# Layer two's softmax weights: transposed by VectorE and POOL's transfers in place of TensorE

## The chip, the cores and the metric

One NeuronCore of one Trainium2 chip runs the kernel. The metric is the device time of one execution in microseconds. Engines: TensorE (PE in the rows, its weight loads PEld), VectorE (DVE), ScalarE (ACT), GpSimd (POOL) and SyncE (SP), each with a queue that it runs in order; they wait for each other on semaphores. L12 is line 12 of the kernel before.

## What is computed

Two layers of a decoder over 256 positions, 2048 features and 16 heads of 128. Layer one has stick-breaking attention, layer two softmax attention against keys and values that are projected behind layer one. With 256 positions and blocks of 256 there is only a query's own block, so layer two's attention is plain causal softmax:

```python
def moba_layer(x, w_in, w_out, k, v, k_mean, pos):
    q, z = jnp.split(x @ w_in, 2, axis=-1)
    o = moba_attention(rope(split_heads(q), pos), k, v, k_mean)
    return (merge_heads(o) * jax.nn.silu(z)) @ w_out
...
        s_own = jnp.where(own_pos[None, :] <= t_idx[:, None], s_own, NEG_BIG)
...
        probs = jax.nn.softmax(scores, axis=-1).astype(v.dtype)
...
        x = layer_norm(DEEPNORM_ALPHA * x + y, ln_g[i], ln_b[i])
        x = x + (p[i] @ w_ple[i]) * jax.nn.sigmoid(x @ w_ple_gate[i])
```

Everything is float32 in and out.

## The kernel before

**Pieces.** All weights stream through the core as pieces of 256 rows by 512 columns (512 KB). SP loads a piece into one of 4 tiles of `raw`; ScalarE rounds it to `w_hi` (`split`, L481), VectorE subtracts to get `w_lo` (L752), both with 8 tiles; TensorE multiplies it in three passes, high by high, high by low, low by high, so twelve matmuls of 128x512 (L1191 to L1193). A chunk is eight pieces, one output of 512 columns, that is four heads; it goes to one half of `acc`, even and odd chunks in turn.

**Slots.** On ScalarE and VectorE `pieces` writes the program of a chunk as eight slots. Slot j first waits until TensorE has used piece j, then splits the piece eight further on; what else must be done at that time stands behind it (`after`) or ahead of it (`before`). SP's load into a tile of `raw` waits until VectorE's low half of the piece four earlier is done. TensorE's own steps stand behind the piece with the same number.

**Layer two's attention.** After the first K chunk come, for each group of four heads, a V chunk and the K chunk of the next group (`w_kv`); the last group's second chunk is the first eight pieces of the output projection (six of column block 0, then two of block 1; the remaining two of block 0 are pieces 12 and 13, of which piece 12 waits for the last group's gated rows). For a group, in order:
- V chunk, behind piece 2: TensorE turns the rotated keys (`k_turn_b`, waits `roped` and `gated`); ScalarE and VectorE copy them as high and low half (L525, L526, L1139).
- Behind pieces 4 and 5: `query_scores` for heads 0 and 1, then 2 and 3. The queries of tile 0 must have been copied to `qT` by POOL (L462).
- `row_max` (mask L790, maximum L1114), `softmax_exp` (L577), `divide` (L1123, L1127) on VectorE, ScalarE, VectorE, for two heads at a time (b = 0 and 1).
- K chunk, behind pieces 0 and 1: `probs_turn` transposes the probabilities with six 128x128 transposes for each b (L1400); ScalarE copies them out of PSUM (`probsT_copies`, L586, L587), VectorE makes the low half (`probs_lo`, L1149).
- Behind pieces 3 and 4: `weigh_values` for b = 0 and 1, three passes and a float32 matmul for the late keys (L1227, L1267).
- VectorE's slot 4: `gate_group` (L829), then, after ScalarE's `gated_hi` (L494), `gated_lo` (L767). Slot 5: `queries_hi_b` and `queries_lo_b` of the next group (L530, L1134).
- VectorE's slot 7: `k_end`, the rotation of the keys just projected, four products and two sums (L1050 to L1061).

**POOL's exchanges.** Elsewhere in the kernel (layer one's queries, keys and gates, layer two's queries, gates and normed rows) a transpose of a 128x1024 tile is made in two steps: VectorE transposes all its 32x32 squares (L773, L1067), and POOL moves the squares' blocks between groups of 32 partitions with 16 transfers (`exchange`, L431). At the end of layer two's attention POOL also starts the reload of the residual (`load_res(1, x2_spill)`, L401), after the last `q_lo`.

## Time and profile before

| | before |
|---|---|
| median of 3 executions | 1143.97 us (1143.33 to 1145.35) |
| the profiled execution, its own time | 1144.15 us |
| its span on the core | 1142.4 us |
| TensorE busy | 1137.7 us (100%) |
| VectorE busy | 746.5 us (65%) |
| ScalarE busy | 590.4 us (52%) |
| POOL busy | 232.7 us (20%) |
| TensorE's granted clock | 1.00 |

The time is that of the whole execution, the span that from the first to the last instruction. A share of busy time is an average over stages; matmuls overlap, so the start of one and of the next say more than its duration. A row of the timeline has the start in us from the span's start, the duration in us, engine, line, operation, what it writes and reads, and in brackets the idle time ahead of it with what ended it.

### The profile page before, as it was taken

The page shows a single profiled execution, that of the slowest core. Times are in us where ns is not written, and L with a number is a line of the kernel's source. Part 1 is how long each engine was busy: PE and PEld are TensorE (multiplying, and loading weights), DVE is VectorE, ACT ScalarE, POOL GpSimd, SP SyncE. Part 2 cuts the span into 40 slices and gives each one's busy share as a digit, 9 for nine tenths or more (in the row PEclk, how much of TensorE's full clock was granted, in tenths as well). Part 3 has the DMA queues.
Part 4 walks back from the last instruction along what each step waited for, and adds up shares of the span by engine and source line. Part 5 has one row for each costly group of instructions (what it writes and reads, how often), then busy time and mean ns, then how long its engine had stood idle before and what let it go on. Part 6 is the DMA issues. An engine that isn't in the chain of part 4 may idle for free.

```text
span 1142.4 us, 15523 instructions
## 1 busy us (share of the span) xinstructions
PE 1137.7 (100%) x5270; PEld 950.4 (83%) x5270; DVE 746.5 (65%) x795; ACT 590.4 (52%) x669; POOL 232.7 (20%) x475
## 2 busy tenths in 40 slices
PE   9999999999999999999999999999999999999998
PEld 8888888888888888888888888888888888888887
DVE  6665556556556566688798775457766667656873
ACT  6574556456546453455354555555454444434641
POOL 1402221330240300003537754320000010000000
PEclk9999999999999999999999999999999999999999
DMA  9776775675675686457787877764555575763671
GB/s 328 251 229 194 212 203 170 204 217 170 182 225 177 202 310 210 135 176 233 242 280 232 254 241 218 225 212 148 175 171 178 165 239 170 256 200 114 192 245 66
DMA packets 126587, 235.67 MB, mean 206 GB/s; under 512 B 13856, under 2 KB 16160, under 8 KB 126032
## 3 DMA queue, kind: packets, MB, share of 16 engines
q1 hardware_dynamic: 109888, 209.22, 58.5%
q0 software_dynamic: 16368, 25.37, 6.8%
q8 instruction: 24, 0.39, 0.1%
q10 hardware_dynamic: 288, 0.52, 0.1%
q14 instruction: 19, 0.16, 0.0%
HBM read 216.71 MB, written 4.19 MB: 193 GB/s over the span
## 4 chain that ended last, share of the span: by engine, by line
PE 100%; DVE 0%; POOL 0%; issue 0%; DVEq 0%; POOLq 0%
PE acc L1191 31%; PE acc L1193 31%; PE acc L1192 31%; PE aux L1227 2%; PE aux L1220 1%; PE aux L1253 1%; PE aux L1267 1%; PE aux L1284 0%; PE aux L1400 0%; PE aux L1193 0%; PE aux L1192 0%; PE aux L1191 0%; PE aux L1242 0%; PE aux L1389 0%; DVE stage L1038 0%; PE aux L1365 0%
## 5 line engine op out<-in xcount | busy, mean ns | idle before, releaser
L752 DVE TENSOR_TENSOR w_lo<-raw,w_hi 128x1024 fp32r<-128x1024 f32 x388 | 470.2, 1222 | 329.3 <-ACT w_hi L481 328.5
L481 ACT ACTIVATE w_hi<-raw 128x1024 fp32r<-128x1024 f32 x388 | 408.9, 1058 | 437.1 <-PE acc L1193 359.3
L1191 PE MATMUL acc<-w_hi,act 128*128 128x512 f32 x1548 | 607.7, 393 | 0.0
L1193 PE MATMUL acc<-w_hi,act 128*128 128x512 f32 x1548 | 603.1, 390 | 0.0
L1192 PE MATMUL acc<-w_lo,act 128*128 128x512 f32 x1548 | 602.5, 389 | 0.0
L1193 PEld LDWEIGHTS acc<-w_hi,act 128*128 128x128 f32 x1548 | 290.5, 188 | 61.6
L1191 PEld LDWEIGHTS acc<-w_hi,act 128*128 128x128 f32 x1548 | 290.8, 188 | 59.0 <-DVE act L767 0.3
L1192 PEld LDWEIGHTS acc<-w_lo,act 128*128 128x128 f32 x1548 | 290.8, 188 | 58.6
L431 POOL DMA_DIRECT2D heads<-big x192 | 93.8, 497 | 275.2 <-DVE big L773 232.1
L431 POOL DMA_DIRECT2D heads<-v_or_z x64 | 31.2, 497 | 52.0 <-DVE v_or_z L773 39.1
L431 POOL DMA_DIRECT2D stage<-v_or_z x48 | 23.6, 499 | 71.9 <-DVE v_or_z L990 44.5
L431 POOL DMA_DIRECT2D heads<-stage x64 | 31.4, 498 | 18.1 <-DVE stage L1079 16.5
L431 POOL DMA_DIRECT2D heads<-heads x64 | 32.1, 510 | 6.3 <-DVE heads L1067 6.1
L416 POOL TENSOR_TENSOR rstd<-var_eps,minus_half 128x2 f32<-128x2 f32 x3 | 2.2, 717 | 142.2 <-DVE var_eps L927 142.2
L494 ACT ACTIVATE act<-stage 128x1024 fp32r<-128x1024 f32 (+1 forms) x12 | 12.7, 1061 | 32.5 <-DVE stage L947 32.5
L462 POOL COPY heads<-big 128x512 f32 x4 | 2.5, 617 | 128.9 <-PE aux L1227 128.9
L577 ACT ACTIVATE heads<-aux,neg_max 128x128 f32<-128x128 f32 (+1 forms) x32 | 13.0, 420 | 23.7 <-DVE neg_max L1114 23.7
L767 DVE TENSOR_TENSOR act<-stage,act 128x1024 fp32r<-128x1024 f32 (+1 forms) x12 | 14.7, 1223 | 9.0 <-ACT act L494 9.0
L773 DVE STREAM_TRANSPOSE big<-acc 128x1024 f32<-128x1024 f32 x12 | 14.9, 1244 | 6.0 <-PE acc L1193 6.0
L947 DVE TENSOR_SCALAR stage<-aux,ln_col 128x256 f32<-128x256 f32 x32 | 15.2, 536 | 0.9 <-PE aux L1220 0.9
L494 ACT ACTIVATE act<-heads 128x1024 f32 (+1 forms) x8 | 8.5, 1062 | 11.7 <-DVE heads L829 11.7
L481 ACT ACT_TABLE_LOAD x9 | 11.5, 1283 | 4.8 <-DMA raw<-in_w_in_a 4.7
(158 smaller groups left out, 649.6 us busy)
## 6 DMA issues: line engine op xcount, KB each, us to landing
raw<-in_w_in_a SPq DMA_DIRECT2D x124, 512.0 KB, 3.9
raw<-in_w_ple_gate SPq DMA_DIRECT2D x64, 512.0 KB, 4.7
raw<-in_w_in_b SPq DMA_DIRECT2D x64, 512.0 KB, 4.7
raw<-in_w_kv SPq DMA_DIRECT2D x64, 512.0 KB, 3.7
raw<-in_w_out_a SPq DMA_DIRECT2D x32, 512.0 KB, 4.7
raw<-in_w_out_b SPq DMA_DIRECT2D x32, 512.0 KB, 4.8
heads<-big POOLq DMA_DIRECT2D x192, 32.0 KB, 3.3
heads<-in_ln_rows POOLq DMA_DIRECT2D x4, 1024.0 KB, 7.9
```

Source lines behind the costliest of these rows:

```text
L431: pool.dma_start(dst[g * SQUARE:(g + 1) * SQUARE, a * HT // NS:(a + 1) * HT // NS], src[a * SQUARE:(a + 1) * SQUARE, g * HT // NS:(g + 1) ...
L481: nc.scalar.activation(w_hi[:, r], raw[:, r % RAWS], ACT.Copy).then_inc(hi_ready, 1)
L494: nc.scalar.activation(quarter(dst[:, 0], c), src, ACT.Copy).then_inc(act_hi, 1)
L577: last = nc.scalar.activation(prob[:, b, h, lo:hi], aux_b[:, 2 * b + h, lo:hi], ACT.Exp, bias=neg_max[:, b, i:i + 1], accum_out=row_sum[:, ...
L752: nc.vector.tensor_tensor(w_lo[:, r], raw[:, r % RAWS], w_hi[:, r].bitcast(F32), ALU.subtract) \
L767: nc.vector.tensor_tensor(quarter(dst[:, 1], c), src, quarter(dst[:, 0], c).bitcast(F32), ALU.subtract).then_inc(act_ready, 1)
L773: nc.vector.transpose(turned_squares(dst), turned_rows(acc_of(parity))).then_inc(chunk_evac, 1)
L947: last = nc.vector.tensor_scalar(dst, part, g, b, ALU.mult, ALU.add)
L1191: nc.tensor.matmul(dst, hi, w_hi[:, r, i], start=begin, stop=False)
L1192: nc.tensor.matmul(dst, hi, w_lo[:, r, i], start=False, stop=False)
L1193: mm = nc.tensor.matmul(dst, lo, w_hi[:, r, i], start=False, stop=end)
L1227: mm = nc.tensor.matmul(dst, lhs(a), rhs(b), start=start and i == 0, stop=True, skip_group_check=True)
```

## The change

The six transposes for each b leave TensorE. VectorE transposes the divided probabilities as 32x32 squares into `probs_turned` (`turn_probs`, for b = 0 in slot 5, for b = 1 ahead of the split of slot 6), and POOL moves them with 16 transfers for each b into `probs_moved`, which lies where `prob` was; `probs_turned` lies over `kT` and half of `qT`. ScalarE rounds the early keys' weights for both b ahead of its split of the K chunk's slot 5 (`probs_hi`), VectorE subtracts there too (`probs_lo`). TensorE weighs for both b behind piece 6. Gate, high and low half, and the next group's queries, move to slot 7. The second two heads' `row_max` moves ahead of the split of slot 5. POOL copies the next group's queries to `qT` after both sets have landed, not after the scores.

```diff
--- before.py
+++ after.py
@@ -168,6 +168,9 @@
         qT = heads[:, HT:2 * HT].rearrange("p (h t) -> p h t", t=T)
         prob = heads[:, 2 * HT:2 * HT + 4 * SC].rearrange("p (b h c) -> p b h c", b=2, c=SC)
         gt = heads[:, 2 * HT + 4 * SC:].rearrange("p (h t) -> p h t", t=T)
+        PW = 2 * SC // (P // SQUARE)
+        probs_turned = [heads[:, b * 2 * SC:(b + 1) * 2 * SC] for b in range(2)]
+        probs_moved = [heads[:, 2 * HT + b * 2 * SC:2 * HT + (b + 1) * 2 * SC] for b in range(2)]
         gain = heads[:, 0:D]
         offset = heads[:, D:2 * D]
         NS = P // SQUARE
@@ -187,6 +190,16 @@
         def turned_squares(ap):
 
             return ap.rearrange("p (b h t c) -> p t h b c", b=NS, h=HG, t=TT)
+
+        probs_turned_x, probs_moved_x = ([squares(ap) for ap in aps] for aps in (probs_turned, probs_moved))
+
+        def probs_rows(b, lo, hi):
+
+            return prob[:, b, :, lo:hi].rearrange("p h (s a c) -> p h s a c", a=NS, c=SQUARE)
+
+        def early_keys(s, b):
+
+            return w1_parts[:, s, b].rearrange("p h (q a c) -> p (h q) a c", a=NS, c=SQUARE)
 
         vz_flat = v_or_z.rearrange("p t n -> p (t n)")
 
...
@@ -423,13 +437,13 @@
             pool.dma_start(cos_sin[:, :, :, :], rope).then_inc(tables_landed, 16)
             pool.dma_start(ln_col[:, :, :, :], ln_cols).then_inc(tables_landed, 16)
 
-            def exchange(turned, count, dst, src, moved):
+            def exchange(turned, count, dst, src, moved, width=HT // NS):
 
                 pool.wait_ge(turned, count)
                 for a in range(NS):
                     for g in range(NS):
-                        pool.dma_start(dst[g * SQUARE:(g + 1) * SQUARE, a * HT // NS:(a + 1) * HT // NS],
-                                       src[a * SQUARE:(a + 1) * SQUARE, g * HT // NS:(g + 1) * HT // NS]) \
+                        pool.dma_start(dst[g * SQUARE:(g + 1) * SQUARE, a * width:(a + 1) * width],
+                                       src[a * SQUARE:(a + 1) * SQUARE, g * width:(g + 1) * width]) \
                             .then_inc(moved, 16)
 
             for g in range(G):
@@ -457,13 +471,19 @@
                 pool.wait_ge(sz_ready, c + G)
                 exchange(chunk_evac, c + (C_Z + 1), gt_flat, vz_flat, z_moved)
             pool.wait_ge(qT_ready, 2 * G)
-            with pool.Fori(0, G) as g:
-                pool.wait_ge(scores_ready, g * 2 + 2 * G)
+            for g in range(G):
+                if g > 0:
+                    for b in range(2):
+                        exchange(p_turned, 2 * g - 1 + b, probs_moved[b], probs_turned[b], p_moved[b], PW)
+                    for b in range(2):
+                        pool.wait_ge(p_moved[b], g * MOVED)
                 nc.gpsimd.tensor_copy(qT[:, :, 0:P], quarter(q_all, g)[:, :, 0:P]).then_inc(q_group_ready, 1)
             pool.wait_ge(q_group_ready, G)
             pool.wait_ge(q_lo, 2 * G)
             pool.wait_ge(x2_spilled, 16 * G)
             load_res(1, x2_spill)
+            for b in range(2):
+                exchange(p_turned, 2 * G - 1 + b, probs_moved[b], probs_turned[b], p_moved[b], PW)
             pool.wait_ge(pv_done, 4 * G)
             load_p(1)
             pool.wait_ge(act_ready, S_OUT[1] + G)
@@ -579,12 +599,11 @@
                                                     accum_out=row_sum[:, b, i:i + 1])
                 last.then_inc(probs_raw, 1)
 
-            def probsT_copies(k, b):
-
-                act.wait_ge(probsT_psum, (k - G) * 2 + (b + 1))
-                s = scores_of(b)
-                nc.scalar.activation(prob[:, b, :, T:SC], s[:, :, T:SC], ACT.Copy).then_inc(w_ready, 1)
-                nc.scalar.activation(w1_parts[:, 0, b], s[:, :, 0:T], ACT.Copy).then_inc(weights_hi, 1)
+            def probs_hi(k, b):
+
+                act.wait_ge(p_moved[b], (k - G) * MOVED + MOVED)
+                nc.scalar.activation(early_keys(0, b), probs_moved_x[b][:, 0:4], ACT.Copy) \
+                    .then_inc(weights_hi, 1)
 
 
             for i, w_sem in enumerate((w_half_landed[0], w_landed[0])):
...
@@ -732,16 +751,19 @@
                 return {2: [lambda: k_copies_b(k)], 4: [lambda: softmax_exp(k, 0)],
                         5: [lambda: softmax_exp(k, 1)], 7: [lambda: values_hi_b(k, n + PC)]}
 
+            def before_k_b(k):
+                return {5: [lambda: probs_hi(k, 0), lambda: probs_hi(k, 1)]}
+
             def after_k_b(k):
-                return {0: [lambda: probsT_copies(k, 0)], 1: [lambda: probsT_copies(k, 1)],
-                        4: [lambda: gated_hi(k, k - G)]}
+                return {7: [lambda: gated_hi(k, k - G)]}
 
             with act.Fori(0, G - 1) as g:
                 n = g * (2 * PC) + (N_KV + PC)
                 pieces(n, N_KV, after_v_b(g + G, n))
-                pieces(n + PC, N_KV, after_k_b(g + G) | {5: [lambda: queries_hi_b(g + (G + 1))]})
+                pieces(n + PC, N_KV, {7: after_k_b(g + G)[7] + [lambda: queries_hi_b(g + (G + 1))]},
+                       before=before_k_b(g + G))
             pieces(N_OUT[1] - PC, N_KV, after_v_b(2 * G - 1, N_OUT[1] - PC))
-            out_ple_gate(1, after_k_b(2 * G - 1))
+            out_ple_gate(1, after_k_b(2 * G - 1), before_k_b(2 * G - 1))
 
 
         @block.vector
...
@@ -1129,6 +1152,14 @@
                         ALU.mult)
                 last.then_inc(probs_ready, 1)
 
+            def turn_probs(k, b):
+
+                dve.wait_ge(probs_ready, (k - G) * 2 + (b + 1))
+                nc.vector.transpose(probs_turned_x[b][:, 0:4].rearrange("p (h q) a c -> p h q a c", q=2),
+                                    probs_rows(b, 0, T))
+                nc.vector.transpose(probs_turned_x[b][:, 4:6], probs_rows(b, T, SC)[:, :, 0]) \
+                    .then_inc(p_turned, 1)
+
             def queries_lo_b(k):
                 dve.wait_ge(q_hi, k + 1)
                 nc.vector.tensor_tensor(q1_parts[:, 1], quarter(q_all, k - G)[:, :, P:T],
@@ -1146,29 +1177,33 @@
 
             def probs_lo(k, b):
                 dve.wait_ge(weights_hi, k * 2 + (b + 1))
-                nc.vector.tensor_tensor(w1_parts[:, 1, b], scores_of(b)[:, :, 0:T], w1_parts[:, 0, b].bitcast(F32),
-                                        ALU.subtract).then_inc(weights_lo, 1)
+                nc.vector.tensor_tensor(early_keys(1, b), probs_moved_x[b][:, 0:4],
+                                        early_keys(0, b).bitcast(F32), ALU.subtract).then_inc(weights_lo, 1)
 
             def after_v_b(k, n):
                 return {2: [lambda: keys_lo_b(k)],
-                        4: [lambda: row_max(k, 0)], 5: [lambda: row_max(k, 1), lambda: divide(k, 0)],
-                        6: [lambda: divide(k, 1)],
+                        4: [lambda: row_max(k, 0)], 5: [lambda: divide(k, 0), lambda: turn_probs(k, 0)],
                         7: [lambda: values_lo_b(k), lambda: evacuate_v(n, 1, v_or_z)]}
 
-            def after_k_b(k):
-                return {0: [lambda: probs_lo(k, 0)], 1: [lambda: probs_lo(k, 1)],
-                        4: [lambda: gate_group(k, k - G, quarter(sz_all, k - G)),
-                            lambda: gated_lo(k, k - G, (k - G) + S_OUT[1])]}
+            def before_v_b(k):
+                return {5: [lambda: row_max(k, 1)], 6: [lambda: divide(k, 1), lambda: turn_probs(k, 1)]}
+
+            def before_k_b(k):
+                return {5: [lambda: probs_lo(k, 0), lambda: probs_lo(k, 1)]}
+
+            def gate_b(k):
+                return [lambda: gate_group(k, k - G, quarter(sz_all, k - G)),
+                        lambda: gated_lo(k, k - G, (k - G) + S_OUT[1])]
 
             pieces(N_KV, N_KV, {5: [lambda: queries_lo_b(G)]} | k_end(N_KV, 0))
             with dve.Fori(0, G - 1) as g:
                 n = g * (2 * PC) + (N_KV + PC)
-                pieces(n, N_KV, after_v_b(g + G, n))
-                pieces(n + PC, N_KV, after_k_b(g + G) | {5: [lambda: queries_lo_b(g + (G + 1))]}
-                       | k_end(n + PC, g + 1))
+                pieces(n, N_KV, after_v_b(g + G, n), before=before_v_b(g + G))
+                pieces(n + PC, N_KV, {7: gate_b(g + G) + k_end(n + PC, g + 1)[PC - 1]
+                                      + [lambda: queries_lo_b(g + (G + 1))]}, before=before_k_b(g + G))
             n = N_OUT[1] - PC
-            pieces(n, N_KV, after_v_b(2 * G - 1, n))
-            out_ple_gate(1, after_k_b(2 * G - 1))
+            pieces(n, N_KV, after_v_b(2 * G - 1, n), before=before_v_b(2 * G - 1))
+            out_ple_gate(1, {7: gate_b(2 * G - 1)}, before_k_b(2 * G - 1))
 
 
         @block.tensor
...
@@ -1392,14 +1427,18 @@
                                       lambda i, h=h: k1_parts[:, i, h], False)
                 mm.then_inc(scores_ready, 1)
 
-            def probs_turn(k, b):
-
-                pe.wait_ge(probs_ready, (k - G) * 2 + (b + 1))
+            def weigh_values_b(k, b, v_chunk):
+
+                pe.wait_ge(weights_lo, k * 2 + (b + 1))
+                pe.wait_ge(v_lo, k + 1)
+                pe.wait_ge(chunk_evac, v_chunk + 1)
                 for i in range(2):
-                    for s in range(3):
-                        mm = nc.tensor.transpose(aux_b[:, 2 * b + i, s * P:(s + 1) * P],
-                                                 prob[:, b, i, s * P:(s + 1) * P], ident[:, :])
-                mm.then_inc(probsT_psum, 1)
+                    head = slice((2 * b + i) * P, (2 * b + i + 1) * P)
+                    o = aux_b[:, 2 * b, i * T:(i + 1) * T]
+                    three_passes(o, lambda part: v1_parts[:, part, head], lambda part: w1_parts[:, part, b, i], i == 0)
+                    mm = nc.tensor.matmul(o[:, P:T], v_or_z[:, 1, head], probs_moved_x[b][:, 4 + i], start=False,
+                                          stop=True, skip_group_check=True)
+                mm.then_inc(pv_done, 1)
 
             chunk(N_Q, N_Q, act1, 0, C_Q, quarters=S_X2, after={2: [last_x2_turn]})
             with pe.Fori(1, 2 * G) as c:
@@ -1410,9 +1449,7 @@
                         5: [lambda: query_scores(k, 1)]}
 
             def after_k_b(k, v_chunk):
-                return {0: [lambda: probs_turn(k, 0)], 1: [lambda: probs_turn(k, 1)],
-                        3: [lambda: weigh_values(k, 0, v_chunk, v1_parts, v_or_z, w1_parts)],
-                        4: [lambda: weigh_values(k, 1, v_chunk, v1_parts, v_or_z, w1_parts)]}
+                return {6: [lambda: weigh_values_b(k, 0, v_chunk), lambda: weigh_values_b(k, 1, v_chunk)]}
 
             chunk(N_KV, N_KV, act0, 0, C_KV, quarters=S_KV)
             pe.wait_ge(sz_ready, 2 * G)
```

Left out: the semaphores (`p_moved` and `p_turned` come, `probsT_psum` goes), the argument by which `out_ple_gate` takes `before_out`, and `weigh_values` of layer one, whose body stays.

The instructions of VectorE at the end of a K chunk, before. L752 is a split, L829 the gate, L767 the low half of the gated rows, L1050 to L1061 the rotation:

```order
L829 TENSOR_TENSOR heads<-aux,big 128x1024
L767 ISA [waits act_operand_hi]
L767 TENSOR_TENSOR act<-heads,act 128x1024
...
L752 TENSOR_TENSOR w_lo<-raw,w_hi 128x1024 [waits act_hi_ready]
L1050 TENSOR_TENSOR heads<-acc,cos_sin 128x8x64 [waits pe_piece_used]
L1051 TENSOR_TENSOR heads<-acc,cos_sin 128x8x64
L1052 TENSOR_TENSOR heads<-acc,cos_sin 128x8x64
L1053 TENSOR_TENSOR heads<-acc,cos_sin 128x8x64
L1058 ISA [waits dve_rope_mul]
L1059 TENSOR_TENSOR heads<-heads 128x8x64 [waits dve_chunk_evac]
L1061 TENSOR_TENSOR heads<-heads 128x8x64
```

And of the change, where L774 is the split, L851 the gate, L789 the low half, and from L1073 the rotation:

```order
L774 TENSOR_TENSOR w_lo<-raw,w_hi 128x1024 [waits act_hi_ready]
L851 ISA [waits pe_pv_done,act_sz_ready]
L851 TENSOR_TENSOR heads<-aux,big 128x1024
L788 REGISTER_ALU
L789 ISA [waits act_operand_hi]
L789 TENSOR_TENSOR act<-heads,act 128x1024
L1073 TENSOR_TENSOR heads<-acc,cos_sin 128x8x64 [waits pe_piece_used]
L1074 TENSOR_TENSOR heads<-acc,cos_sin 128x8x64
L1075 TENSOR_TENSOR heads<-acc,cos_sin 128x8x64
L1076 TENSOR_TENSOR heads<-acc,cos_sin 128x8x64
L1080 REGISTER_ALU
L1081 ISA [waits dve_rope_mul]
```

The gate and its low half, with the wait for ScalarE's high half (`act_operand_hi`) between them, stood behind the split of slot 4; now they stand behind that of slot 7, ahead of the rotation; the low half of the next group's queries (L1134, now L1165) follows behind the rotation.

POOL from the gates' exchanges on, before (the copy stands in a loop over the four groups):

```order
L431 DMA heads<-v_or_z 32x256 x64
L460 UNCONDITIONAL_BRANCH
L460 ISA
L462 ISA
L462 COPY heads<-big 128x4x128
L460 REGISTER_ALU
L460 COMPARE_AND_BRANCH
L401 DMA big<-x_spill 128x2x512 x4
L406 DMA stage<-in_pt 128x2x256
```

And of the change, its last two groups:

```order
L480 COPY heads<-big 128x4x128
L445 DMA heads<-heads 32x192 x32
L480 COPY heads<-big 128x4x128
L415 DMA big<-x_spill 128x2x512 x4
L445 DMA heads<-heads 32x192 x32
```

Two sets of 16 transfers now lie behind each copy (the first three pairs stand above these rows in the same way), and the reload of the residual (`big<-x_spill`) lies between the last copy and the last two sets.

TensorE in the K chunk, behind the last matmul of piece 6, in the change (the transposes behind pieces 0 and 1 and the weighing behind 3 and 4 are gone):

```order
L1228 MATMUL acc<-w_hi,act 128x512
L1432 ISA
L1434 REGISTER_ALU [waits dve_v_lo,dve_weights_lo]
L1262 MATMUL aux<-act,v_parts 128x256 [waits dve_chunk_evac]
L1262 MATMUL aux<-act,v_parts 128x256 x2
L1439 MATMUL aux<-heads,v_or_z 128x128
L1262 MATMUL aux<-act,v_parts 128x256 x3
L1439 MATMUL aux<-heads,v_or_z 128x128
L1432 REGISTER_ALU
L1262 MATMUL aux<-act,v_parts 128x256 [waits dve_chunk_evac,dve_v_lo,dve_weights_lo]
L1262 MATMUL aux<-act,v_parts 128x256 x2
L1439 MATMUL aux<-heads,v_or_z 128x128
```

Each of the two steps waits for the low half of its own two heads (`dve_weights_lo`); the second follows the first with no piece between.

## Rows read from the trace of the kernel before

**Rows 1.** The page, chain that ended last, by engine.
```profile
PE 100%; DVE 0%; POOL 0%; issue 0%; DVEq 0%; POOLq 0%
```

**Rows 2.** Windows, first group: us, engines' busy us (instructions), PEclk, DMA share, GB/s.
```profile
769.30:819.90 50.60, 50.60 (x254) 42.72 (x253) 34.79 (x42) 26.12 (x42) 0.61 (x1) 1.00 0.51 161
```

**Rows 3.** Timeline of PE: start us, us, engine, line, operation, tiles, shapes, count.
```profile
777.32 1.04 PE L1220 MATMUL aux<-ident,heads 128*128 128x128 f32 x8
...
793.97 0.39 PE L1193 MATMUL acc<-w_hi,act 128*128 128x512 f32 x1
...
796.69 0.39 PE L1193 MATMUL acc<-w_hi,act 128*128 128x512 f32 x1
...
796.92 0.82 PE L1400 MATMUL aux<-ident,heads 128*128 128x128 f32 x6
...
800.10 0.39 PE L1193 MATMUL acc<-w_hi,act 128*128 128x512 f32 x1
...
806.22 0.39 PE L1193 MATMUL acc<-w_hi,act 128*128 128x512 f32 x1
...
806.45 0.52 PE L1227 MATMUL aux<-act,v_parts 128*128 128x256 f32 x3
...
807.53 0.48 PE L1191 MATMUL acc<-w_hi,act 128*128 128x512 f32 x1
...
810.15 0.39 PE L1193 MATMUL acc<-w_hi,act 128*128 128x512 f32 x1
...
819.53 0.39 PE L1193 MATMUL acc<-w_hi,act 128*128 128x512 f32 x1
```

**Rows 4.** Timeline of DVE, then line L1067: duration ns min/median/max.
```profile
791.74 0.69 DVE L790 TENSOR_TENSOR aux<-aux,future 128x512 f32<-128x512 f32 x1
...
793.40 0.17 DVE L1123 RECIPROCAL row_sum<-row_sum 128x4 f32<-128x4 f32 x1
...
793.60 1.03 DVE L1127 TENSOR_TENSOR heads<-heads,row_sum 128x256 f32<-128x256 f32 x2
...
812.87 1.22 DVE L829 TENSOR_TENSOR heads<-aux,big 128x1024 f32<-128x1024 f32 x1
...
815.46 1.23 DVE L767 TENSOR_TENSOR act<-heads,act 128x1024 f32 x1 [1.37 <-ACT act L494]
...
821.11 1.23 DVE L752 TENSOR_TENSOR w_lo<-raw,w_hi 128x1024 fp32r<-128x1024 f32 x1 [1.49 <-ACT w_hi L481]
...
822.25 0.68 DVE L1050 TENSOR_TENSOR heads<-acc,cos_sin 128x512 f32<-128x512 f32 x1
...
825.37 0.68 DVE L1061 TENSOR_TENSOR heads<-heads 128x512 f32<-128x512 f32 x1
...
919.59 1.23 DVE L752 TENSOR_TENSOR w_lo<-raw,w_hi 128x1024 fp32r<-128x1024 f32 x1
...
L1067 DVE STREAM_TRANSPOSE heads<-heads x4: 1245/1245/1247, 601.5 to 666.7; 128x1024 f32<-128x1024 f32 x4
```

**Rows 5.** Timeline of POOL, then DMA issues: KB each, median us to landing.
```profile
689.12 7.81 POOL L431 DMA_DIRECT2D heads<-v_or_z  x16 [12.84 <-issue]
...
789.07 0.61 POOL L462 COPY heads<-big 128x512 f32 x1 [28.97 <-PE aux L1227]
...
920.22 2.88 POOL L401 DMA_DIRECT2D big<-x_spill  x4 [29.33 <-DVE q_parts L1134]
...
raw<-in_w_out_b SPq DMA_DIRECT2D x32, 512.0 KB, 4.8
...
heads<-heads POOLq DMA_DIRECT2D x64, 32.0 KB, 3.6
```

**Rows 6.** Timeline of ACT, then line L510: duration ns min/median/max.
```profile
700.42 1.28 ACT L560 ACT_TABLE_LOAD   x1 [0.73 <-DMA heads<-v_or_z]
...
930.72 1.06 ACT L481 ACTIVATE w_hi<-raw 128x1024 fp32r<-128x1024 f32 x1 [3.00 <-DMA raw<-in_w_out_b]
...
L510 ACT ACTIVATE big<-heads x4: 613/632/633, 66.0 to 348.3; 128x512 f32<-128x512 f32 x4
```

22 lines of the change are left out of this document (12 added, 10 removed).

## Prediction

> **What bounds the kernel now.** I read the chain of waits first: every part of it that counts is TensorE [rows 1]. Then the windows, one for each group of four heads in layer two: 50.60 us long, TensorE busy for all of it, at a granted clock of 1.00 [rows 2]. So whatever leaves TensorE's queue there shortens the run, and whatever makes TensorE wait there lengthens it, and nothing else counts. All other numbers come from the timelines of one group, from 769.3 to 819.9 us; a span of 50.60 us repeats it.
>
> In TensorE's timeline [rows 3] a piece of twelve matmuls takes 2.72 us (793.97 to 796.69). I call the V chunk's pieces V0 to V7 and the K chunk's K0 to K7; 793.97 is the last matmul of V7, 819.53 that of K7.
>
> **What leaves TensorE.** A piece with six transposes behind it takes 3.41 us (796.69 to 800.10), so six cost 0.69. The six behind K1 cost about the same. Eight such steps: 8 x 0.68 = 5.4 us saved, all on the path. The weighing stays, four steps of it less: a step costs 810.15 - 806.22 - 2.72 = 1.21 us, of which its own matmuls are 807.53 - 806.45 = 1.08; the other 0.13 is the passage back to wide matmuls, which two steps in a row pay once: 4 x 0.13 = 0.5 us saved. ScalarE and VectorE also lose or swap copies of equal size (two of 128x256 go, two of 128x512 move); that lies beside TensorE's work and is priced at nothing.
>
> **What is added beside it.** In each group VectorE gets two times a transpose of 128x512 and one of 128x256. The nearest row is 1.245 us for 128x1024 [rows 4]; by elements, with 0.18 us fixed, that is 0.71 and 0.45, about 1.04 us one after the other. VectorE has over 15 us idle in each window [rows 2], so only its place in the chain of the softmax matters. POOL gets 32 issues a group.
>
> **First wait: the weights must be back before the weighing.** I follow the chain in the first group's times.
> 1. The scores of the second two heads are there when POOL's copy wakes, 789.07 [rows 5]. VectorE now masks them and takes their maximum at once: 793.40 - 791.74 = 1.66 us [rows 4], so 790.7. Then the split of slot 5 (1.14, 821.11 to 822.25), the division of the first two heads (0.20 + 1.03) and the two transposes (1.04): 794.1.
> 2. POOL needs 16 issues for each set. One set took 7.81 us of issues [rows 5], two 15.65. It wakes some 0.5 us after a transpose has ended; so the last issue ends at about 810.4. The second two heads are transposed by 796.5, long before POOL can take them.
> 3. From the end of the last issue (689.12 + 7.81 = 696.93) to the reader's start at 700.42 [rows 5, 6] 3.5 us passed. The 3.6 us median from issue to landing [rows 5] gives 3.2. Where traffic is low it may be half of that. I take 3.0 (range 1.7 to 3.5): ScalarE starts at 813.4.
> 4. ScalarE rounds 128x512 in 0.63 [rows 6], VectorE subtracts in about 0.7, with some 0.1 us of signals twice: 815.0.
> TensorE wants the second step at 793.97 + 7 x 2.72 + 0.23 + 1.08 = 814.3. The first step is ready in time, as its set lands 8 us earlier. So TensorE stands still for 0.6 us in each group, 4 x 0.6 = 2.4 us in all; between 0 (1.7 us in point 3) and 1.2 each (3.5 us), so 0 to 4.8.
> The wait in front of slot 5 holds up ScalarE's splits behind it, three of them by up to 3 us, and VectorE's with them; these feed pieces eight later, 21.8 us, and reach nobody.
> A sentence apart: the Trainium skill, DMA: Bandwidth & Descriptors, section on the anatomy of a SWDGE transfer, fits 2.0 us plus bytes over 436 GB/s, which for 24 KB is 2.1 us; the trace has 3.6 for transfers of 32 KB, and the measurement decides. By the page's figure the first wait would vanish and the estimate would be 2.4 us lower.
>
> **Second wait: the gate is now in front of the rotation.** Call U the end of K7 (819.53 + 0.39 = 819.92). Before, VectorE split at 821.11, rotated the keys from 822.25 and was done at 825.37 + 0.68 = 826.05, so U + 6.1 [rows 4]. TensorE turns these keys behind V2, at 777.32 + 50.60 = 827.92, U + 8.0 [rows 3]. The margin was 1.9 us. The weighing behind K6 pushes gate and low half out of slot 4 into slot 7, ahead of the rotation. From the gate's start to that of the low half 2.59 us pass, in which VectorE waits for ScalarE's high half, then 1.14 for the low half itself [rows 4]: 3.7 us. The keys are rotated at U + 9.9. TensorE waits 1.9 us, and its weight load can't run ahead any more, 0.2: 2.1 us. It happens behind the K chunks of the first three groups (the very first K chunk has no gate ahead, and behind the fourth group nothing is rotated): 3 x 2.1 = 6.3 us lost. Bounds: 5.6 (no restart cost) and 6.9. Late next are the low halves of the turned keys, wanted behind V4; by the same addition they are ready at U + 15.1 where TensorE comes at U + 16.7: no further wait.
>
> **Third: what POOL has moved.** The 2 MB of the residual (four issues at 920.22 [rows 5], U - 0.9 of the third group) wait for the last low half of the queries, which now comes behind the rotation, U + 10.6. They now meet the weights for slots 4 and 5 of the last V chunk. Before, they delayed ScalarE by 3.00 us at 930.72 [rows 6], where the softmax was not yet running. Now the same squeeze lies on it. The raw tile for slot 4 is freed by the low half of slot 0, U + 11.6. At the usual 4.8 us from issue to landing [rows 5] it is there at U + 16.4, with a third more at U + 18; ScalarE wants it at U + 17.1. Before, the tile read at 930.72 had been freed at 919.59 + 1.23 = 920.82 [rows 4], 9.9 us earlier; at that rate it is U + 21.5. I take the nearer end, since this tile has no other queued in front of it: the last group's exponentials, set and weighing come 1.0 us later (0 to 4.4). POOL's copy of the queries now stands behind both sets (about 814), but its readers come behind V4 at about U + 16.7, over 20 us later.
>
> **The sum:** - 5.4 - 0.5 + 2.4 + 6.3 + 1.0 = + 3.8 us. The profiled execution took 1144.15 us around a span of 1142.4; the median is 1143.97, 0.2 below, and I put the sum on the median: **1147.8 us**. By the bounds alone, from - 5.9 + 5.6 = - 0.3 to - 5.9 + 4.8 + 6.9 + 4.4 = + 10.2.
>
> **Rivals.**
> - *The sets land quickly.* With 1.7 us from the last issue to the reader, the first wait is gone: 1147.8 - 2.4 = 1145.4. For it: a transfer is a quarter smaller than those of the rows. Against it: the weight stream runs at the same time, as it did at 700.42. The second wait is untouched.
> - *The last group is squeezed harder.* If the residual's 2 MB take the larger share and the raw tile of slot 4 lands 4.4 us late, as the 9.9 us in front of 930.72 make thinkable, the third term is 4.4 and not 1.0: 1147.8 + 3.4 = 1151.2.
> - *Faster: the rotation keeps its old place in time.* The mechanism of the second wait would have to fail: it decides at whether the rotated keys are signalled by U + 8.0. If VectorE could do gate and low half under waits that it has anyway, the sum is 3.8 - 6.3 = - 2.5, so 1141.5; with quick landings as well 1139.1. For it: VectorE is idle for a third of the window. Against it: in slot 7 there is no idle time ahead of the rotation, which followed the split directly (821.11, 822.25), and its engine runs in order.
> - *It doesn't give back the transposes.* If TensorE hides part of them in its pipeline, 5.4 shrinks; but the pieces' ends are 3.41 apart and not 2.72, so I give this next to nothing.
>
> **How the numbers follow.** My forecast 0.50, quick landings 0.20, harder squeeze 0.15, faster 0.12, the last 0.03. A measurement of this kernel can tell about 0.2% from no change, 2.3 us. Slower are the forecast, the squeeze and the last (0.50 + 0.15 + 0.03), less 0.03 for a forecast whose terms all fall low: 0.65. Within: quick landings (+ 1.4) and these 0.03, 0.23. Faster: 0.12. The range reaches from 1142.8, which leaves out most of the faster case, to 1151.4, which takes in the squeeze, and leaves out about 2 in 10.
>
> **What would show it.** TensorE idle, in the profile after, in front of the turning of the keys, about 2 us, three times, put down to VectorE's rotation; TensorE idle in front of the second weighing step of each group, 0.6 us, put down to VectorE's subtraction and behind that to POOL's transfers; windows of the middle groups 50.60 - 1.5 + 2.1 + 0.6 = 51.8 us long; the clock still 1.00. Window lengths of about 49.1 us would prove me wrong: then no wait was there. No idle time at the keys but a longer one at the weighing would mean that the sets, not the gate, are the price.

## The result, and the profile after

The changed kernel took **1153.69 us** (median of 6 runs, 1152.56 to 1155.86), the kernel before 1144.21 beside it: ratio 1.0085, 95% interval 1.0075 to 1.0095. It is 9.5 us slower. Forecast were + 3.8 us, with a range to 1151.4: the direction was right, the size wrong.

The page, where [rows 1] had TensorE for the whole chain:

```profile
span 1152.0 us, 15541 instructions
...
PE 1135.7 (99%) x5222; PEld 947.6 (82%) x5222; DVE 754.0 (65%) x811; ACT 588.4 (51%) x661; POOL 295.2 (26%) x603
...
PE 91%; POOL 3%; DVE 2%; DMA 2%; issue 1%; ACT 1%; DVEq 0%; ACTq 0%; POOLq 0%
```

The rest of the chain is now POOL's issues, VectorE and transfers. The windows, bounded where TensorE's steps stand (columns as in [rows 2]):

```profile
819.10:870.30 51.20, 49.37 (x242) 41.44 (x241) 36.73 (x46) 25.74 (x41) 16.23 (x33) 1.00 0.55 178
870.30:923.30 53.00, 49.59 (x242) 41.47 (x241) 36.73 (x46) 25.72 (x41) 16.23 (x33) 1.00 0.54 173
923.30:980.00 56.70, 50.42 (x235) 42.20 (x234) 36.71 (x46) 24.05 (x39) 19.27 (x37) 0.94 0.62 203
```

TensorE now has idle time in each: 1.8, 3.4 and 6.3 us. In the last the clock is 0.94. The waits of TensorE (us in total, times, longest) name two places:

```profile
PE aux L1262 <- DVE act L1180: 6.1, 2, 4.5
PE aux L1255 <- DVE heads L1084: 5.4, 3, 1.8
```

L1255 turns the keys, L1084 is the rotation's last sum; L1262 weighs, L1180 is the low half of the weights. TensorE's timeline at these places:

```profile
814.53 0.60 PE L1262 MATMUL aux<-act,v_parts 128*128 128x256 f32 x3
...
815.11 0.60 PE L1262 MATMUL aux<-act,v_parts 128*128 128x256 f32 x3
...
815.69 0.48 PE L1226 MATMUL acc<-w_hi,act 128*128 128x512 f32 x1
...
826.46 0.39 PE L1228 MATMUL acc<-w_hi,act 128*128 128x512 f32 x1
828.68 1.09 PE L1255 MATMUL aux<-ident,heads 128*128 128x128 f32 x8 [1.83 <-DVE heads L1084]
...
916.77 0.38 PE L1439 MATMUL aux<-heads,v_or_z 128*128 128x128 f32 x2
918.73 0.62 PE L1262 MATMUL aux<-act,v_parts 128*128 128x256 f32 x3 [1.58 <-DVE act L1180]
...
932.82 1.09 PE L1255 MATMUL aux<-ident,heads 128*128 128x128 f32 x8 [1.75 <-DVE heads L1084]
...
969.72 0.38 PE L1439 MATMUL aux<-heads,v_or_z 128*128 128x128 f32 x2
974.63 1.01 PE L1262 MATMUL aux<-act,v_parts 128*128 128x256 f32 x3 [4.53 <-DVE act L1180]
975.44 0.63 PE L1439 MATMUL aux<-heads,v_or_z 128*128 128x128 f32 x2
...
976.78 0.77 PE L1226 MATMUL acc<-w_hi,act 128*128 128x512 f32 x1
...
977.78 0.63 PE L1228 MATMUL acc<-w_hi,act 128*128 128x512 f32 x1
```

**The account.** What an interruption costs is the distance between the starts on either side of it, less the usual distance (0.23 us between wide matmuls, 0.14 from one weighing step to the next).
- Turning of the keys: starts 2.22, 2.22 and 2.14 us apart, so 2.0 + 2.0 + 1.9 = 5.9 us.
- Second weighing step: none in the first two groups; 918.73 - 916.77 - 0.14 = 1.8 us in the third, 974.63 - 969.72 - 0.14 = 4.8 us in the last. Together 6.6.
- Clock: granted 0.5 (1.2 GHz) from 973.1 to 979.9 us, beginning within the wait of 4.5 us. The second step takes 976.78 - 974.63 = 2.15 us where it took 815.69 - 814.53 = 1.16 in the first group, and seven wide matmuls start about 0.43 us apart and not 0.23: 1.0 + 1.4 = 2.4 us.
- Saved, as forecast: 5.4 + 0.5.

The sum is - 5.9 + 5.9 + 6.6 + 2.4 = + 9.0 us, of 1152.0 - 1142.4 = 9.6 between the spans. The remaining 0.6 I could not put down to a place.

**Why the second step was late in the third and last group.** POOL's timeline, with its four pairs of sets:

```profile
794.55 15.62 POOL L445 DMA_DIRECT2D heads<-heads  x32 [34.20 <-DVE heads L1160]
845.74 15.62 POOL L445 DMA_DIRECT2D heads<-heads  x32 [31.98 <-DVE heads L1160]
898.53 15.62 POOL L445 DMA_DIRECT2D heads<-heads  x32 [33.51 <-issue]
933.97 2.87 POOL L415 DMA_DIRECT2D big<-x_spill  x4 [15.92 <-DVE q_parts L1165]
951.91 13.71 POOL L445 DMA_DIRECT2D heads<-heads  x28 [15.07 <-DVE heads L1160]
966.63 1.96 POOL L445 DMA_DIRECT2D heads<-heads  x4 [1.00 <-issue]
```

and ScalarE's rounding of the second set, its reader, in the four groups:

```profile
813.04 0.63 ACT L605 ACTIVATE act<-heads 128x512 fp32r<-128x512 f32 x1 [2.90 <-DMA heads<-heads]
...
864.30 0.63 ACT L605 ACTIVATE act<-heads 128x512 fp32r<-128x512 f32 x1 [3.17 <-DMA heads<-heads]
...
917.33 0.63 ACT L605 ACTIVATE act<-heads 128x512 fp32r<-128x512 f32 x1 [4.99 <-DMA heads<-heads]
...
973.22 0.63 ACT L605 ACTIVATE act<-heads 128x512 fp32r<-128x512 f32 x1 [7.80 <-DMA heads<-heads]
```

From POOL's last issue to the reader it is 813.04 - (794.55 + 15.62) = 2.9, then 2.9, 3.2 and, from 966.63 + 1.96 = 968.59, 4.6 us. VectorE's transposes of the third group's first set ended at 896.63:

```profile
896.23 0.40 DVE L1160 STREAM_TRANSPOSE heads<-heads 128x256 f32<-128x256 f32 x1
```

POOL began at 898.53, 1.9 us later, where it took 0.3 us in the other three groups, and the wait is marked "issue": it waited for nothing that the profile shows. In the last group a gap of 1.0 us of the same kind lies inside the second set, the set starts late, and the transfers land late.

The set starts late there because a load of a weight piece stood in front of the softmax for 11.40 us; the chain of waits has it (the duration stands in second place), and ScalarE's split behind it:

```profile
935.66 11.40 DMA raw<-in_w_out_b
...
947.08 1.06 ACT L501 ACTIVATE w_hi<-raw 128x1024 fp32r<-128x1024 f32 x1 [1.07 <-DMA raw<-in_w_out_b]
```

The residual's four transfers were issued from 933.97 to 936.84 us, at the same time. They were not in the queues any more when the last set landed, some 20 us later: the last of them had landed by 948.8 us (last start 936.1, + 0.7 of issue, + 11.9 at most), by the rows of their tile:

```profile
L415 POOL DMA_DIRECT2D big<-x_spill x4: 706/724/734, 934.0 to 936.1; - x4
...
DMA to landing us min/median/max: 4.7/9.3/11.9
```

### The profile page after: what moved, and what is told of

Same layout as the page of the kernel before. It is cut to its first block, busy times and chain, and to the rows that moved or that the text cites. A ratio compares the mean times of both kernels' runs of the same rounds, so it can differ in the third digit from the quotient of the medians.

```text
span 1152.0 us, 15541 instructions
## 1 busy us (share of the span) xinstructions
PE 1135.7 (99%) x5222; PEld 947.6 (82%) x5222; DVE 754.0 (65%) x811; ACT 588.4 (51%) x661; POOL 295.2 (26%) x603
## 4 chain that ended last, share of the span: by engine, by line
PE 91%; POOL 3%; DVE 2%; DMA 2%; issue 1%; ACT 1%; DVEq 0%; ACTq 0%; POOLq 0%
PE acc L1226 28%; PE acc L1228 28%; PE acc L1227 28%; POOL heads L445 3%; PE aux L1262 2%; DMA raw<-in_w_out_b 1%; PE aux L1255 1%; DMA heads<-heads 1%; PE aux L1288 1%; PE aux L1319 0%; DVE w_lo L774 0%; ACT w_hi L501 0%; DVE heads L851 0%; PE aux L1228 0%; PE aux L1227 0%
## 5 line engine op out<-in xcount | busy, mean ns | idle before, releaser
L774 DVE TENSOR_TENSOR w_lo<-raw,w_hi 128x1024 fp32r<-128x1024 f32 x388 | 468.9, 1222 | 312.3 <-ACT w_hi L501 311.7
L445 POOL DMA_DIRECT2D heads<-heads x192 | 94.6, 501 | 122.1 <-DVE heads L1160 81.2
L789 DVE TENSOR_TENSOR act<-stage,act 128x1024 fp32r<-128x1024 f32 (+1 forms) x12 | 14.7, 1223 | 9.0 <-ACT act L514 9.0
L1180 DVE TENSOR_TENSOR act<-heads,act 128x512 fp32r<-128x512 f32 x8 | 5.5, 689 | 16.2 <-ACT act L605 16.2
L1262 PE MATMUL aux<-act,v_parts 128*128 128x256 f32 x48 | 9.9, 323 | 6.1 <-DVE act L1180 6.1
L605 ACT ACTIVATE act<-heads 128x512 fp32r<-128x512 f32 x8 | 5.0, 623 | 18.9 <-DMA heads<-heads 18.9
```

The lines of the kernel that those rows point to most:

```text
L445: pool.dma_start(dst[g * SQUARE:(g + 1) * SQUARE, a * width:(a + 1) * width], src[a * SQUARE:(a + 1) * SQUARE, g * width:(g + 1) * width]) \
L774: nc.vector.tensor_tensor(w_lo[:, r], raw[:, r % RAWS], w_hi[:, r].bitcast(F32), ALU.subtract) \
L789: nc.vector.tensor_tensor(quarter(dst[:, 1], c), src, quarter(dst[:, 0], c).bitcast(F32), ALU.subtract).then_inc(act_ready, 1)
L1262: mm = nc.tensor.matmul(dst, lhs(a), rhs(b), start=start and i == 0, stop=True, skip_group_check=True)
```

## The experiments

Each ratio is to the kernel before in the same session (1144.0 in the first, 1143.88 us in the other two). The code of the edits is abbreviated: `gate`, `queries_lo` and the like stand for the steps of that name, and an edit of VectorE's slots that ScalarE's slots repeat is shown once.

**Before, with the gate moved behind the piece's last slot.** The transposes stay on TensorE; gate, high and low half go to slot 7, ahead of the rotation:

```
-  pieces(n + PC, N_KV, after_k_b(g + G) | {5: queries_lo} | k_end(n + PC, g + 1))
+  steps = after_k_b(g + G); gate = steps.pop(4)
+  pieces(n + PC, N_KV, steps | {5: queries_lo, 7: gate + k_end(n + PC, g + 1)[PC - 1]})
```

> The kernel before with one edit: the gate, its high and its low half move from slot 4 to slot 7, ahead of the rotation; transposes, copies and weighing stay where they were. Theory A (the gate ahead of the rotation costs TensorE 2 us at each of three turnings of the keys, whatever became of the transposes): 6 us on top of the kernel before, 1150 to 1151 us, with three waits of 1.8 us put down to VectorE's rotation. Theory B (the keys are late only together with the sets, the earlier maximum or the later weighing): 1144 to 1145 us and no such wait.

1150.39 us, ratio 1.0058 (1.0041 to 1.0075), + 6.4 us. Its TensorE waits at the keys three times, like the changed kernel:

```profile
PE aux L1224 <- DVE heads L1063: 5.4, 3, 1.8
```

So the second wait alone, without any set of transfers, costs 6.4 us, where 6.3 were forecast.

**Before, with twelve transposes for six.** Each step on TensorE is made twice:

```
-  for s in range(3):
+  for s in (0, 1, 2, 0, 1, 2):
```

> The kernel before with each of its eight transpose steps on TensorE doubled: the same six transposes of 128x128 are made twice into the same place, twelve in all (the result is the same). Theory A: transposes lie fully on TensorE's path, so this costs what the change was reckoned to give back: 8 x 0.69 = 5.5 us at most, 8 x 6 transposes at the pitch inside a step about 4.6 to 5.5 us: 1148.6 to 1149.5. Rival B: TensorE hides them, under 1 us: 1144 to 1145.

1148.92 us, ratio 1.0042 (1.0025 to 1.0059): + 5.0 us for 48 more transposes. They lie on TensorE's path: added, they cost 5.0 us where 5.4 were reckoned for taking them away.

**The reload of the residual behind the last sets.**

```
-  load_res(1, x2_spill)
   for b in range(2):
       exchange(p_turned, 2 * G - 1 + b, ...)
+  load_res(1, x2_spill)
```

> The change with one edit: POOL starts the reload of the residual behind the last two sets of transfers. Theory A (the last group's wait of 4.5 us and the fall of the clock behind it come from the reload's 2 MB, which meet the weights ahead of the softmax): ScalarE's waits for raw tiles in slots 4 and 5 of the last V chunk go, the last wait falls to 0 to 2 us, the granted clock stays at 1.00, and 5 to 7 us come off: 1147 to 1149 us. Theory B (the last group waits because the output projection's own stream is heavier, or because POOL's sets are late whatever else runs): the last wait and the clock's fall stay, 1153 to 1154 us.

1147.92 us, ratio 1.0031 (1.0019 to 1.0042), 5.8 us less than the changed kernel. The keys' wait is unchanged; of the other, 6.1 us in the changed kernel, the rest is

```profile
PE aux L1262 <- DVE act L1180: 2.3, 3, 1.5
```

The second step of the last group waits 0.47 us, and the clock stays at 1.00. There the set starts 17.4 us behind the turning of the keys (933.60 to 951.00), with the reload ahead 19.1 (932.82 to 951.91); from the last issue to the reader it is 3.3 us and not 4.6; and POOL's 1.0 us falls behind the sets. The three make 1.7 + 1.3 + 1.0 = 4.0 us of the 4.8. Why the landing was 1.3 us longer is not shown. The residual had landed by then in the changed kernel; what differs is the weight stream: in the 2 us behind the last issue the DMA engines were busy for 0.92 of the time there and for 0.77 here. The step's start comes 3.3 us earlier than in the changed kernel (971.35), the end 5.7 us: the clock was worth the other 2.4 us. The Trainium skill, TensorE: Matmul & The Clock Gate, section Terms, prices a stretch at the lower clock at half its length; by that the estimate for 6.8 us is 3.4. TensorE stood still for the first 1.5 us of it (973.1 to 974.63), and half of the other 5.3 is 2.6: the trace agrees if only the worked part is counted.

**The second weighing step behind piece 7.**

```
-  return {6: [weigh b = 0, weigh b = 1]}
+  return {6: [weigh b = 0], 7: [weigh b = 1]}
```

> The change with one edit: TensorE takes the second weighing step behind piece 7 in place of behind piece 6. Theory A: the wait of 1.6 us in the third group goes, the last one falls from 4.5 to about 2 us and with it the clock's fall (2.7 us); the keys' three waits shrink by 1.1 us each, since TensorE now has 1.2 us more to do between piece 7 and the turning of the keys; the passage back to wide matmuls is paid once more, 0.5 us. 1.8 + 2.7 + 2.7 + 3.3 - 0.5 = 10 us off: 1143 to 1145 us. Theory B (the wait at the keys hangs on the end of the weighing, since the gate waits for it): the keys' waits stay at 1.8 us, and only 6 to 7 us come off, 1146.5 to 1148 us.

1142.18 us, ratio 0.9986 (0.9976 to 0.9995): this one edit takes 11.5 us away. It gives up the 0.5 us of the merged passage. The waits of TensorE are

```profile
PE aux L1255 <- DVE heads L1084: 1.9, 3, 0.7
...
PE aux L1262 <- DVE act L1180: 1.0, 1, 1.0
```

It is 0.8 us below the range that I expected: the last group's wait fell to 1.0 us and not to about 2. The keys' wait fell from 2.0 to 0.8 us, 1.2 each where 1.1 was expected. The step of 1.2 us now stands behind the chunk's last piece: slot 7 of VectorE begins while TensorE is at it, since the gate, which needs its result, comes behind a split; and TensorE still passes it before the keys. VectorE's split ahead of the gate, in the timeline after,

```profile
819.88 1.23 DVE L774 TENSOR_TENSOR w_lo<-raw,w_hi 128x1024 fp32r<-128x1024 f32 x1 [2.86 <-ACT w_hi L501]
```

starts 2.1 us earlier here (817.78), and TensorE is ready for the keys only 0.9 us earlier (826.59 - 0.8 = 825.8 against 828.68 - 2.0 = 826.7): 1.2 us more room.

**The rotation ahead of the gate.**

```
-  {7: gate_b(g + G) + k_end(n + PC, g + 1)[PC - 1] + queries_lo}
+  {7: k_end(n + PC, g + 1)[PC - 1] + gate_b(g + G) + queries_lo}
```

> The change with one edit: in VectorE's slot 7 the rotation comes ahead of the gate and its low half. Theory A (each wait of TensorE is a loss of its own): the three waits of 1.8 us in front of the turning of the keys go, with their 0.2 us of restart each, 6.0 us; but the low halves of the turned keys come within some 0.3 us of their deadline, and in the last group TensorE is 2 us further when the squeezed raw tile lands, so its wait at the second weighing step grows from 4.5 to 6 or 7 us. Net 3 to 5 us off the changed kernel: 1149 to 1151 us. Theory B (the sets of transfers are the only price, and the waits at the keys only take up slack that the weighing would use): the waits at the second weighing step grow in every group by what the keys' waits lose, and the time stays at 1153 to 1154 us.

1153.77 us, ratio 1.0083 (1.0066 to 1.01): nothing gained. Theory A's range is missed by 2.8 us; theory B has the time but not the place, for the waits at the weights grew only from 6.1 to 6.7 us. The waits at the keys are gone, and others stand in their place:

```profile
PE aux L1262 <- DVE act L1180: 6.7, 2, 4.7
PE aux L1424 <- DVE act L1170: 3.9, 3, 1.7
```

L1424 are the scores, L1170 the low half of the turned keys. VectorE's timeline shows why:

```profile
826.50 1.23 DVE L789 TENSOR_TENSOR act<-heads,act 128x1024 f32 x1 [1.36 <-ACT act L514]
...
829.26 3.50 DVE L774 TENSOR_TENSOR w_lo<-raw,w_hi 128x1024 fp32r<-128x1024 f32 x3 [0.94 <-ACT w_hi L501]
832.68 1.22 DVE L1170 TENSOR_TENSOR act<-aux,act 128x1024 fp32r<-128x1024 f32 x1
```

Gate and queries now keep VectorE and ScalarE until 829, the three splits of the next pieces pile up to 3.5 us, and the low half of the keys behind them ends where it ended in the changed kernel (832.48 + 1.22), while TensorE arrives 2 us earlier. The scores start 2.04, 2.07 and 0.99 us behind the matmul ahead of them, 4.4 us more than usual in all: of 5.9 us won 1.5 are left. The profiled execution loses these again: 0.6 us more at the weights, and a clock that fell twice, for 3.4 us after the third group's wait and again around the last group's.

**Rotation first and the reload last.** The two edits shown, together.

> The change with two edits: the rotation ahead of the gate in VectorE's slot 7, and the residual's reload behind the last two exchanges; the second weighing step stays behind piece 6. Theory A (what the trace of the kernel with the rotation first shows): of the 6.0 us won in front of the turned keys about 4.4 go again in front of the scores, which want the turned keys' low half (1.8, 1.8 and 0.8 us); so it stands 1.6 us below the kernel with the reload alone (1147.9): 1146.3, and up to 1147.5 if the granted clock again falls for 3.4 us after the third group's wait. Rival B: the rotation first was worth its 6 us and only the last group's squeeze hid it: 1142 to 1143, and no TensorE idle in front of the scores.

1148.15 us (1145.43 to 1148.74), ratio 1.0031 (1.0018 to 1.0044), against 1147.92 with the reload alone. Rival B falls: TensorE waits at the scores for 4.0 us in three waits, and in front of the third group's second step for 2.3. The 1.6 us of theory A are not shown. Its two executions with a mean clock of 1.00 took 1145.43 and 1146.0 us, near its 1146.3; the four with 0.998 or 0.999 took 1148.14 to 1148.74, more than the 1147.5 that it allowed for a fall of the clock. The kernel with the reload alone spreads as widely, from 1145.56 to 1148.11.

**Rotation first and the second step behind piece 7.** Here VectorE also waits for both weighing steps ahead of the rotation.

> The change with two edits: the rotation ahead of the gate in VectorE's slot 7, and the second weighing step behind piece 7; the residual's reload stays ahead of the last two exchanges. Theory A: the two do not get in each other's way, since the step behind piece 7 gives the turned keys' low half 1.2 us more room; the 2.3 us in front of the keys in the kernel with the second step behind piece 7 (1142.2) go, and at most 1 us comes back in front of the scores: 1140 to 1141, the last group's wait of 1.0 us still there. Rival B: the low half is late as before, 1.8 us in each group: 1142 to 1144.

1143.68 us (1141.51 to 1148.54), ratio 1.0 (0.9987 to 1.0013): a miss for theory A by 2.7 us, 1.5 us above the second step behind piece 7 alone, and within rival B's range, whose 1.8 us in front of the scores are not there. Its profile shows where the time went. The keys give 2.4 us by the starts. The two waits at the scores take 1.2 us by the starts (0.9 by the waits, as expected). The last group's second step waits 1.9 us and not 1.0, since with the reload still ahead of the sets TensorE, arriving earlier, meets the same late landing: 1.0 us. And the clock, which had stayed at 1.00 in the other kernel, fell to 0.5 from 969.4 to 972.9 us, beginning 0.7 us after this wait, which by the starts cost 1.6 us. That is - 2.4 + 1.2 + 1.0 + 1.6 = + 1.4. Of the spread of 7 us among its executions the two slowest, 1146.29 and 1148.54, have the lowest mean clock, 0.997; the rest stays unexplained.

**All three edits.** In one kernel slot 7 of VectorE has the order rotation, gate, queries' low half, gated low half:

```
+  {7: wait pv_done, rotation, gate, queries_lo, gated_lo}      (ScalarE: queries_hi, gated_hi)
```

in the other the low half of the queries stays last and ScalarE's slot as the change has it.

> The change with three edits together: the second weighing step behind piece 7 instead of piece 6, the residual's reload behind the last two exchanges, and in slot 7 of VectorE the rotation of the keys first, then gate, low half of the queries, low half of the gated rows (ScalarE's slot 7 turned round to fit: queries' high half ahead of the gated rows'). Theory A: the losses are the three waits and the clock and nothing else. The kernel with the second step behind piece 7 took 1142.18 us; left in its trace are 0.8 us in front of each of three turnings of the keys (2.3 us) and 1.1 us in front of the last group's second step. Rotation first takes the 2.3, the reload the 1.1: 1138.8 us, span 1136.6, no TensorE idle over 0.5 us in layer two's attention, clock 1.00. Rival B: as in the kernel with the rotation first alone, the wait only moves to the scores, which want the low half of the turned keys (1.0 to 1.8 us each there): then 1141 to 1142 us, with TensorE idle in front of the scores.

**1138.67 us**, ratio 0.9954 (0.9938 to 0.9971): 15.0 us below the changed kernel and 5.2 below the kernel before. Theory A, 1138.8. TensorE has no idle time in the groups, where the changed kernel had 1.8 and 3.4 us in these two windows:

```profile
819.10:870.30 51.20, 51.20 (x250) 42.91 (x249) 38.62 (x50) 25.64 (x40) 16.28 (x33) 1.00 0.58 184
870.30:923.30 53.00, 53.00 (x258) 44.44 (x257) 40.16 (x52) 25.76 (x41) 16.28 (x33) 1.00 0.56 181
```

> As the kernel of the three edits together, but slot 7 of VectorE in the order rotation, gate, low half of the gated rows, low half of the queries, and ScalarE's slot 7 left as the change has it. Theory A: the order behind the rotation doesn't matter, since the turned keys' low half has 1.2 us more room than in the kernel with the rotation first alone: 1138.8 us, as the other. Rival B: VectorE's wait for ScalarE's high half of the gated rows (1.4 us before) holds up its splits and so the turned keys' low half; TensorE then waits in front of the scores 0.5 to 1 us in three groups, 1140.5 to 1142 us.

1139.97 us, ratio 0.9966 (0.9952 to 0.9981). TensorE waits at the scores for 0.9 us in two groups. Rival B's mechanism at a smaller size: 1.3 us for the order behind the rotation.

**POOL's late starts: instructions or transfers?** First 48 tiny fills more on POOL, where it is idle:

```
+  for i in range(48): nc.gpsimd.memset(pool_spare[:, i:i + 1], 0.0)
```

> The change with 48 more tiny fills on POOL (one column each, of a spare tile) behind its first copy of the queries, where it would otherwise stand idle for some 30 us. They lengthen POOL's program by 48 instructions and nothing else. Theory A: POOL's two late starts (1.9 us in front of the third group's second set, 1.0 us inside the last group's second set) belong to positions in its program: they move to transfers 48 instructions earlier, so the third group's second step no longer waits for them (TensorE idle there falls from 1.6 us to 0.3 or less), and the late start is seen elsewhere in POOL's rows. Rival B: they belong to what else runs at that time (the weight stream, the other engines): they stay in front of the same transfers at about 896 us and 966 us, and TensorE's wait stays 1.6 us. Time within 2 us of the change's under either.

One run, 1153.35 us. Theory A falls: the third group's set starts at 898.50 after "issue" and the gap of 1.0 us is at 967.14, both in front of the same transfers as before, the 510th and 574th when POOL's transfers are counted from the start of the program. Rival B is not shown by it: with all three edits the gap stands at 958.96, in front of the residual, which there is the 574th transfer. So I added transfers, 16 in a spare tile, with a wait of POOL for them after every four:

```
+  for i in range(16):
+      nc.gpsimd.dma_start(pool_spare[..., 1], pool_spare[..., 0]).then_inc(spare_moved, 16)
```

> The change with 16 more transfers on POOL behind its first copy of the queries, of the same form as those of the sets (32 rows of 768 bytes) and within a spare tile, where POOL would otherwise stand idle for some 30 us; nothing waits for them but POOL itself. The two late starts of POOL sat at its 510th and 574th transfer in every kernel so far (in one of them the 574th was the residual's and not a set's). Theory A: it is the count of transfers that decides. The 510th is now the first of the second group's second set: the late start moves there, near 846 + 8 = 854 us, the third group's set starts some 0.5 us after its transposes as in the others, and TensorE's 1.6 us in front of the third group's second step go to 0.3 or less, while the second group's second step waits for 0.5 to 1 us. The 574th is then the 13th transfer of the last group's first set, near 958 us. Rival B: it is the place in the group or the time: the third group's set still starts 1.9 us late, near 898.5 us, and TensorE's wait stays 1.6 us.

One run, 1152.8 us. POOL's timeline:

```profile
846.35 7.83 POOL L448 DMA_DIRECT2D heads<-heads  x16 [32.52 <-DVE heads L1171]
855.00 7.83 POOL L448 DMA_DIRECT2D heads<-heads  x16 [0.82 <-issue]
...
898.63 15.66 POOL L448 DMA_DIRECT2D heads<-heads  x32 [31.90 <-DVE heads L1171]
...
966.67 1.97 POOL L448 DMA_DIRECT2D heads<-heads  x4 [1.46 <-issue]
```

The first late start moved with the count: it is again in front of the 510th transfer, now the second set of the second group. There TensorE's second step comes 1.6 us late (starts 1.70 apart), and in the third group, whose set starts 0.3 us after its transposes, it waits no more. The second late start did not move: it is in front of the 590th transfer now. What they have in common, and what POOL does in them, stays open. In this kernel, with the reload ahead of the sets too, the last set took only 3.3 us from its last issue (966.67 + 1.97) to the reader at 971.93; the DMA engines were busy for 0.46 of the 2 us behind that issue.

## Why the prediction was wrong

- **Transposes and passage, - 5.9:** right. From one turning of the keys to the next it is 51.20 us (828.68 to 879.88), that is 50.60 - 1.5 + 2.1; doubling the transposes cost 5.0 against 5.4.
- **Second wait, + 6.3:** right in place, cause and size: 5.9 by the starts, 6.4 when made alone in the kernel before. "Late next are the low halves of the turned keys", with 1.6 us of room, was right for the changed kernel (ready at 832.48 + 1.22, the scores start at 835.08: 1.4 us), but that room was also all that putting the rotation first could give: the kernel with that edit waits there.
- **First wait, + 2.4:** right in the landing time, wrong in its form. I gave all four groups one landing time, 3.0 us (measured 2.9, 2.9, 3.2), and one wake-up of POOL, some 0.5 us (measured 0.3). In the first two groups the low half was ready 0.1 us before TensorE came (813.71 + 0.69 against 814.53), so the step cost 0 and not 0.6 each; with the reload last, where the first group's copy behind the sets woke 3.6 us after the last issue (814.00 against 794.75 + 15.62), it waited 0.33 us. In the third POOL started 1.6 us later than usual and the step cost 1.8. That start belongs to a count of transfers, as the 16 more transfers showed; before, POOL issues only 452 transfers. But the trace of before has such gaps too, and I had not looked for them: 1.1 and 1.2 us at 548 and 644 us, in front of POOL's 228th and 330th transfers, where nobody waits, and one in [rows 5] itself. The row at 689.12 us, the 382nd transfer, says "issue"; VectorE's transpose had ended at 684.60 + 1.24 = 685.84, 3.3 us earlier, where the next exchange took 0.55 us.

```profile
684.60 1.24 DVE L773 STREAM_TRANSPOSE v_or_z<-acc 128x1024 f32<-128x1024 f32 x1
```

  The rival of quick landings had the cost of the two first groups right, though not their landing time (2.9 us and not 1.7), and nothing else.
- **Third, + 1.0 (0 to 4.4):** this is the step that failed. It moved the softmax of the last group by the delay of one raw tile, and ended there. That delay was 1.7 us. But with the reload ahead the set itself also landed later, 4.6 us after its last issue and not 3.3, for a reason that is not shown (the residual had landed some 20 us earlier), and POOL lost 1.0 us within the set. First and third term together were 3.4 forecast and 6.6 measured, 4.8 of it in the last group, where 0.6 + 1.0 were forecast. The rival of the harder squeeze (4.4 in the third term) came near the size of this wait, 4.8, by luck: its reason was a raw tile 4.4 us late, and that delay was 1.7.
- **The clock:** missing altogether. The forecast wrote "the clock still 1.00"; around a wait of 4.5 us it was 0.5 for 6.8 us, which cost 2.4 us by the starts and 2.4 by the comparison with the reload last. Both readings are from single profiles, and of the six executions of the changed kernel the one with the highest mean clock, 0.999, took 1154.37 us, so a smaller fall did not make it faster. "The bounds alone" reach + 10.2, above the result, without this term; the stated range ended at 1151.4, with the squeeze as its worst case, and so below the result.
- The faster rival fell, as expected: VectorE has no idle time ahead of the rotation.

By account: 0.4 us too much at the keys, 3.2 too little at the weights, 2.4 at the clock: + 3.8 - 0.4 + 3.2 + 2.4 = + 9.0.

## What to carry over

A merged step gains its passage once and can lose much more: the place of TensorE's steps decides how late their operands may be, and one line (the second step one piece later) was worth 11.5 us, about twice the 5.9 us that the detour through VectorE and POOL saves on TensorE. Follow a large transfer past the tile that it first meets, to every step that this tile holds up: put behind the last sets, this one was worth 5.8 us. When a forecast holds a wait of several us on TensorE, give the clock a term of its own.

## What was not expected of the hardware

- POOL, ready to issue, began 1.9 us after the transposes (usually 0.3), and 1.0 and 0.8 us late between two transfers, with nothing in the profile to wait for, in front of the same transfers in every kernel with the detour but that with 16 more; 48 more instructions did not move this, 16 more transfers moved one of two.
- The granted clock fell around a wait of 4.5 us and in no kernel after the waits of 1.8 us at the keys. But in the kernel with the rotation first it fell for 3.4 us after a wait at the weights that kept two starts 2.3 us apart, and in the kernel with that and the second step behind piece 7, again for 3.4 us after starts 2.3 apart. With the rotation first and the reload last it did not fall after starts 2.7 apart, nor in the third group with 48 tiny fills, where they were 2.8 apart.
- From a set's last issue to its reader it took 2.3 to 4.0 us in the first three groups of all kernels with the detour. In the last group it took 2.9 to 3.6 in the four kernels with the reload behind the sets, and 4.2 to 4.6 in five of the six with it ahead, but 3.3 in the sixth, that with 16 more transfers. So the reload ahead does not always lengthen the landing. By the fit of the Trainium skill, DMA: Bandwidth & Descriptors, Anatomy of one DMA, the estimate for a transfer of 24 KB is 2.1 us; no set here was that quick, and the measurement decides.
- VectorE's transpose of 128x512 took 0.71 us as estimated, 128x256 0.40 (estimated 0.45).
